# A dense layer and attention projections: from three fp32r matmuls on split operands to plain fp32 on four tiles of 32 columns

## The chip, the cores and the metric

The kernel runs on one core of one Trainium2 chip. The metric is the device time of one execution in microseconds (us), the median of several runs. The two kernels are "before" and "after". TensorE (PE) does the matmuls, VectorE (DVE) and ScalarE (ACT) work element by element, GpSimd (POOL) does small arithmetic and issues some transfers, and SyncE (SP) issues the weight loads.

## What is computed

A trunk of two layers on one sequence of 256 tokens with 1024 channels, everything in float32:

```python
mod_all = einsum('bd,lde->lbe', silu(c), w_mod) + b_mod     # adaLN: 6 vectors of 1024 for each layer
h = rms_norm(x, norm_g[i, 0]) * (1 + scale1) + shift1
y = pool_mixer(h)                  # layer 0
y = diff_attention(h)              # layer 1: h @ w_qkv (1024 x 3072), 8 heads, ..., @ w_o (1024 x 1024)
x = x + gate1 * rms_norm(y, norm_g[i, 1])
h = rms_norm(x, norm_g[i, 2]) * (1 + scale2) + shift2
y = (silu(g) * u) @ w_down         # layer 0: g, u = split(h @ w_gu); D_FF = 2816, the dense layer
y = moe_swiglu(h)                  # layer 1: top 2 of 8 experts, each 3584 wide
x = x + gate2 * rms_norm(y, norm_g[i, 3])
```

The change concerns three parts: the dense layer (`ffn_w_gu`, `ffn_w_down`), attention's input projections (`w_qkv`), and its output projection (`w_o`).

## The kernel before, in words

**Order of the work.** The head computes four pieces of layer 0's adaLN on TensorE (20 units of `w_mod`, `head_units`, L1889) together with the pooling mixer. Then come the dense layer in 11 steps of 256 channels of D_FF, attention with its projections, the router, and the eight experts. The order on each engine is written out by hand; engines meet at semaphores.

**Weight units.** All weights ahead of the experts come in units of 1 MB (128 x 2048 floats, two transfers each) into the buffer `raw`, which has `RAW` = 6 slots. The SP queue issues them in one fixed order (`load`, L530); a unit's load waits until the unit six places ahead of it has been done (`unit_done`). Besides the 20 of the head there are 22 units of gate and up, 11 of the down projection, 12 of queries, keys and values, 4 of the output projection, and 28 later adaLN units, which VectorE multiplies by silu(c) and adds up in `rows` (`gemv_unit`, L1259, two operations a unit): 20 during the dense layer and 8 during the input projections (`FFN_MODS`, `QKV_MODS`). A gate and up unit has 4 of the 8 blocks of 128 input channels and 256 columns of each of the two.

**Splitting.** A float32 operand a is split in two fp32r parts: ScalarE writes the high part (`high`, L860, into `whi`), VectorE subtracts (`low`, L1250, into `wlo`, and counts `unit_done`). Three slots (`SPL` = 3) hold split units. The activations are split likewise: the normalized input into `thi` and `tlo` (L943, L1370 and `modulate_tile`, L975, `low_pair`, L1467), the product of silu and up into `ahi` and `alo`. TensorE then makes each product of three matmuls:

```python
pe.matmul(out, a_hi, b_hi, start=start, stop=False, ...)   # L1873
pe.matmul(out, a_hi, b_lo, start=False, stop=False, ...)   # L1874
pe.matmul(out, a_lo, b_hi, start=False, stop=stop, ...)    # L1875
```

For gate and up (`ffn_gate_up`, L2013), queries and keys (`qkv_group`, L2108) the weights are stationary, 128 x 128, and the input of 256 tokens moves; a product has 256 columns. A step of gate and up is 8 channel blocks x 2 x 2 = 32 products, a group of queries or keys 32 as well. For the down projection (`ffn_down`, L2035, `down_tile`, L2063), the values (L2125 and `last_values`, L2147) and the output projection (L2222) the activation of 128 tokens is stationary and 512 columns of the weights move; these are 8 products a step, 16 for each half of the values, and 32 for the output projection. Step s of the dense layer is gate and up of chunk s+1 and then down of chunk s.

**Around it.** Sixteen bf16 matmuls of zeros clear the down banks after the first step (`zero_bank`, L1877), and 24 keep TensorE busy just before the dense layer (`keep_clock`, L1884). `row_sum` (L1854) adds up a row of `rows` over the partitions with two fp32 matmuls of 512 columns; that of shift 3 (`row_sum(1, 3)`, L2106) stands ahead of the values. The norm ahead of attention ends in full transposes (`turn_normalized`, L2093), whose results ScalarE scales and shifts. In attention TensorE alternates scores, transposes of the weights, the last values' matmuls and the products with the values (L2196 to L2219). `project_low` (L1514) makes the low part of the output weights; the first at the end of the input projections, the other three after the last heads. GpSimd waits for them all (L774) before it clears the experts' sums in HBM (L781).

**Experts.** The ring of 16 slots for expert weights (`ring`, L299) is laid over `raw`, the split buffers and others; loads into it start as the slots become free (L601 to L622). The experts already use plain fp32: the 96 gathered tokens are stationary, 32 at a time, and each of four column tiles of the array (`tile_out`, L358) reads its own quarter of the weights as moving columns: 448 for gate and up (L2359, L2370), 256 for down (L2384). A gate or an up pass is 8 x 3 x 4 = 96 matmuls, a down pass 14 x 3 x 4 = 168; there are 16 of each, and after the last down pass the results are scattered. `gather` (L2307) opens the stage.

Of the kernel before, what the change touches and what calls it, by code (L numbers as in the profile page):

```python
# [34 lines left out]
RAW = 6  # L35
SPL = 3
UNIT = 2048
FC = 256
NCF = FF // FC
# [16 lines left out]
FFN_MODS = [[], [(1, 0, 0), (1, 0, 1)], [(1, 0, 2), (1, 0, 3)], [(1, 1, 0), (1, 1, 1)], [(1, 1, 2), (1, 1, 3)],  # L56
            [(0, 5, 0), (0, 5, 1)], [(0, 5, 2), (0, 5, 3)], [(1, 2, 0), (1, 2, 1)], [(1, 2, 2), (1, 2, 3), (1, 3, 0)],
            [(1, 3, 1), (1, 3, 2), (1, 3, 3)]]
QKV_MODS = [[], [(1, 4, 0), (1, 4, 1)], [(1, 4, 2), (1, 4, 3)], [(1, 5, 0), (1, 5, 1)], [(1, 5, 2), (1, 5, 3)], []]

QKV_ORDER = (4, 0, 1, 2, 3, 5)

R_FFN, Q_FFN = len(HEAD), 0


HT_PARTS = KC
# [4 lines left out]


def ffn_steps():

    r, q, n, steps = R_FFN + 2, 2, 0, []
    for s in range(NCF - 1):
        steps.append((s, r, q, FFN_MODS[s], n))
        r, q, n = r + 3 + len(FFN_MODS[s]), q + 3, n + len(FFN_MODS[s])
    return steps, r, q, n


FFN_STEPS, R_LAST_DOWN, Q_LAST_DOWN, N_QKV_MODS = ffn_steps()
R_QKV, Q_QKV = R_LAST_DOWN + 1, Q_LAST_DOWN + 1
R_GROUP = [R_QKV + 2 * g + sum(len(m) for m in QKV_MODS[:g]) for g in range(6)]
R_WO, Q_WO = R_GROUP[5] + 2, Q_QKV + 12
R_MOE, Q_MOE = R_WO + 4, Q_WO + 4
# [18 lines left out]
ROW_ORDER = [[2, 5], [3, 2, 4, 5]]  # L105

ROW_BANK = [[None, None, 0, None, None, 2], [None, None, 0, 2, 6, 6]]
# [69 lines left out]
def build_trunk(nc, x, c, w_mod, b_mod, norm_g, pool_w, pool_scale, w_qkv, w_o, subln_g, lambda_vecs,  # L177
# [10 lines left out]
    with ExitStack() as ctx:  # L188
# [6 lines left out]
        def early(name, shape, dt=F32):  # L195
            return before_experts.enter_context(nc.sbuf_tensor(name, shape, dt))


# [3 lines left out]
        with ExitStack() as at_first:  # L202
            ring_w = at_first.enter_context(nc.sbuf_tensor("ring_w", [P, 2 * SPL, UNIT], F32))
        whi = sb("whi", [P, SPL, UNIT], F32R)
        wlo = sb("wlo", [P, SPL, UNIT], F32R)
# [5 lines left out]
        thi = sb("thi", [P, UNIT], F32R)  # L211
        tlo = sb("tlo", [P, UNIT], F32R)
        with ExitStack() as at_first:
            act_in = at_first.enter_context(nc.sbuf_tensor("act_in", [P, GROUPS * QUARTER], F32))
        ahi = sb("ahi", [P, 512], F32R)
        alo = sb("alo", [P, 512], F32R)
# [30 lines left out]
        thi3 = thi[:, :].rearrange("p (k s) -> p k s", k=KC)  # L247
        tlo3 = tlo[:, :].rearrange("p (k s) -> p k s", k=KC)
# [3 lines left out]
        last_hi, last_lo = thi[:, 0:512], tlo[:, 0:512]  # L252
# [5 lines left out]
        actf = tmp[:, 512:1024]  # L258
# [20 lines left out]
        before_experts = ExitStack()  # L279
        rows = early("rows", [P, 7, D])  # L280
        scr = early("scr", [P, 6 * D])
        ysb = early("ysb", [P, T, D])
        gain = early("gain", [P, 2, D])
        before_experts.close()
        whx0 = sb("whx0", [P, UNIT], F32R)
        wlx0 = sb("wlx0", [P, UNIT], F32R)
        sb("row4", [P, D])
        whx1 = sb("whx1", [P, UNIT], F32R)
        whx2 = sb("whx2", [P, UNIT], F32R)
        sb("scr_mid", [P, 2 * D])  # L290
        sb("scr_end", [P, UNIT])
        wlx1 = sb("wlx1", [P, UNIT], F32R)
        wlx2 = sb("wlx2", [P, UNIT], F32R)


        o_hi = [whx1[:, :]] + [whi[:, (Q_WO + i) % SPL, :] for i in range(SPL)]
        o_lo = [whx0[:, :]] + [wlo[:, (Q_WO + i) % SPL, :] for i in range(SPL)]
        halves = rows[:, :, :].rearrange("p r d -> p (r d)")
        ring = [raw[:, (R_MOE + i) % RAW, :] for i in range(RAW)] + [halves[:, 5 * D:7 * D]]  # L299
        for i in range(SPL):  # L300
            ring += [ring_w[:, h * SPL + (Q_WO + i) % SPL, :] for h in range(2)]
# [15 lines left out]
        hv = tmp[:, 0:UNIT]  # L317
        hv3 = hv.rearrange("p (k s) -> p k s", k=KC)

# [64 lines left out]
        hi_ready = sem("hi_ready")  # L384
# [19 lines left out]
        first_hi = sem("first_hi")  # L404
        first_lo = sem("first_lo")
# [8 lines left out]
        ht_v = sem("ht_v")  # L414
# [24 lines left out]
        ht_hi = sem("ht_hi")  # L439
        ht_lo = sem("ht_lo")  # L440
# [15 lines left out]
        f_ahi = sem("f_ahi")  # L456
        f_alo = sem("f_alo")
        qkv_ready = sem("qkv_ready")
        values_lo = sem("values_lo")
# [10 lines left out]
        ot_hi = sem("ot_hi")  # L470
        ot_lo = sem("ot_lo")
# [50 lines left out]

        block = ctx.enter_context(nc.Block())
# [5 lines left out]
        def _(sp):  # L529
            def load(r, rounds, halves):  # L530
# [5 lines left out]
                dst = raw[:, r % RAW, :]  # L536
                for view, src in halves(dst):
                    sp.dma_start(view, src).then_inc(raw_loaded[r % RAW], 16)
# [8 lines left out]
            def gu_unit(w, width, chunk, kh):  # L547

                def halves(dst):
                    v = dst.rearrange("p (k g j) -> p k g j", k=4, g=2)  # L550
                    src = w.rearrange("(k p) f -> p k f", p=P)
                    for g in range(2):
                        yield v[:, :, g, :], src[:, kh * 4:kh * 4 + 4, bass.ds(chunk * FC + g * width, FC)]
                return halves
# [18 lines left out]
            for r, (g, pair) in enumerate(HEAD):  # L573
                load(r, 0, mod_unit(0, g, pair))
# [5 lines left out]

            w_gu, w_dn = ffn_w_gu[0], ffn_w_down[0]
            load(R_FFN, 0, gu_unit(w_gu, FF, 0, 0))
            load(R_FFN + 1, 0, gu_unit(w_gu, FF, 0, 1))

            for s, r, _, mods, _ in FFN_STEPS:
                load(r, 0, gu_unit(w_gu, FF, s + 1, 0))
                load(r + 1, 0, gu_unit(w_gu, FF, s + 1, 1))
                for i, mod in enumerate(mods):
                    load(r + 2 + i, 0, mod_unit(*mod))
                load(r + 2 + len(mods), 0, down_unit(w_dn, s))  # L590
            load(R_LAST_DOWN, 0, down_unit(w_dn, NCF - 1))

            for g in range(6):
                for kh in range(2):
                    load(R_GROUP[g] + kh, 0, col_unit(w_qkv[0], QKV_ORDER[g] * 512, kh))
                for i, mod in enumerate(QKV_MODS[g]):
                    load(R_GROUP[g] + 2 + i, 0, mod_unit(*mod))
            for u in range(4):
                load(R_WO + u, 0, col_unit(w_o[0], u % 2 * 512, u // 2))

            def experts(ps_no):  # L601
                u0 = ps_no * NE * EXPERT_UNITS

                def unit(m, e, later, last, src):

                    i = m % RING
                    if ps_no == 0 and m < RING and not last:
                        if i < RAW:
                            sp.wait_ge(unit_done, R_MOE + i - RAW + 1)
                        elif i == RAW:  # L610
                            sp.wait_ge(unit_used, Q_WO + 1)
                        elif i < RAW + 1 + 2 * SPL:
                            sp.wait_ge(unit_used, Q_WO + 2 + (i - RAW - 1) // 2)
                        elif i == RAW + 1 + 2 * SPL:
                            sp.wait_ge(gated, 2 * T + 2)
                        elif i == RAW + 2 + 2 * SPL:
# [1860 lines left out]
```

## Time and profile before

| | |
|---|---|
| median of 3 runs | 1281.88 us (1278.13 to 1283.09) |
| span of the profiled execution, first to last instruction | 1281.1 us (the page gives no other time for it) |
| mean granted clock of TensorE | 0.993 |
| TensorE busy | 1254.9 us (98%) |
| VectorE busy, ScalarE busy | 377.8 us (29%), 214.9 us (17%) |
| moved by DMA | 477.49 MB, mean 373 GB/s |

The profile is of one execution. A busy TensorE is the union of its matmuls, whose ends are modelled; start times are recorded, so the length of a stage or the distance of two starts is the surer measure. Lines L... are those of the kernel before. In a row of the groups by line, "x480" is the number of records and the number after the comma the mean length of one in ns.

### The profile page before, as it was taken

How to read it: one execution, taken by the hardware profiler on the slowest of the kernel's cores; microseconds unless marked ns; L12 is line 12 of the kernel's file. 1: busy time of each engine (PE TensorE's matmuls, PEld its weight loads, DVE VectorE, ACT ScalarE, POOL GpSimd, SP SyncE). 2: the span in 40 equal slices, each digit the busy share in tenths (PEclk: the TensorE clock that was granted, in tenths of full speed). 3: DMA queues.
4: the chain of work that ended last, by engine and by line, in shares of the span. 5: the costliest groups of instructions: out<-in, count | busy, mean ns of one | idle time of the engine just before them, and what ended most of it. 6: DMA issues, size and time to landing. Idle time of an engine off the chain costs nothing.

```text
span 1281.1 us, 31424 instructions
## 1 busy us (share of the span) xinstructions
PE 1254.9 (98%) x14709; PEld 783.7 (61%) x14709; DVE 377.8 (29%) x584; ACT 214.9 (17%) x321; POOL 110.1 (9%) x134
## 2 busy tenths in 40 slices
PE   6899999999999999999999999999999999999997
PEld 3589999989775355545455454554545555454555
DVE  0367877979873110101101011110101201011012
ACT  2353334474742000000000000000000000000001
POOL 2330000010030000020010010002001000200100
PEclk9899999999999999999999999999999999999999
DMA  9998998959369999999999999999999999999980
GB/s 373 387 363 293 325 327 309 374 189 392 150 215 421 424 424 424 424 405 423 425 405 424 424 411 408 424 410 403 424 420 397 421 424 409 405 424 418 397 356 36
DMA packets 114056, 477.49 MB, mean 373 GB/s; under 512 B 10944, under 2 KB 37280, under 8 KB 113792
## 3 DMA queue, kind: packets, MB, share of 16 engines
q1 hardware_dynamic: 106112, 457.29, 89.0%
q0 software_dynamic: 7664, 17.87, 4.5%
q8 instruction: 117, 1.92, 0.5%
q10 hardware_dynamic: 144, 0.26, 0.1%
q14 instruction: 19, 0.16, 0.0%
HBM read 465.79 MB, written 11.16 MB: 372 GB/s over the span
## 4 chain that ended last, share of the span: by engine, by line
PE 95%; DVE 2%; POOL 1%; ACT 1%; issue 0%; DMA 0%; DVEq 0%; ACTq 0%; POOLq 0%
PE ps L2384 23%; PE ps L2370 23%; PE ps L2359 23%; PE ps L1873 7%; PE ps L1874 7%; PE ps L1875 7%; PE ps L1897 2%; PE ps L1988 1%; PE ps L1857 1%; DVE wlo L1518 1%; PE ps L2168 1%; PE ps L1933 0%; DMA scr<-onehot_in 0%; PE ps L1962 0%; PE ps L2313 0%
## 5 line engine op out<-in xcount | busy, mean ns | idle before, releaser
L1745 DVE TENSOR_TENSOR act_in<-act_in,ps 128x1344 f32<-128x1344 f32 x16 | 24.9, 1554 | 526.8 <-PE ps L2370 526.8
L1873 PE MATMUL ps<-thi,whi 128*128 128x256 f32 x480 | 136.0, 283 | 0.7 <-DVE wlo L1367 0.7
L1874 PE MATMUL ps<-tlo,whi 128*128 128x256 f32 x480 | 135.8, 283 | 0.0
L1875 PE MATMUL ps<-thi,wlo 128*128 128x256 f32 x480 | 135.8, 283 | 0.0
L2359 PE MATMUL ps<-raw,turned_in 128*32 128x448 f32 x1296 | 123.7, 539 | 0.0
L2370 PE MATMUL ps<-ring_w,turned_in 128*32 128x448 f32 x1248 | 120.6, 539 | 0.0
L2384 PE MATMUL ps<-ring_w,turned_act 128*32 128x256 f32 x2016 | 117.2, 379 | 0.0
L2384 PE MATMUL ps<-raw,turned_act 128*32 128x256 f32 x2016 | 115.5, 379 | 0.0
L1183 ACT ACTIVATE act_in<-ps 128x1344 f32<-128x1344 f32 x16 | 20.7, 1292 | 548.6 <-PE ps L2359 548.6
L2384 PEld LDWEIGHTS ps<-raw,turned_act 128*32 128x32 f32 x2016 | 82.5, 110 | 33.4 <-issue 3.5
L1253 DVE TENSOR_TENSOR wlo<-raw,whi 128x2048 fp32r<-128x2048 f32 x41 | 92.9, 2289 | 32.8 <-ACT whi L866 32.8
L2359 PE MATMUL ps<-ring_w,turned_in 128*32 128x448 f32 x1056 | 102.6, 539 | 0.0
L2384 PEld LDWEIGHTS ps<-ring_w,turned_act 128*32 128x32 f32 x2016 | 81.2, 110 | 30.2 <-issue 3.1
L2370 PE MATMUL ps<-raw,turned_in 128*32 128x448 f32 x1008 | 96.2, 539 | 0.0
L1873 PEld LDWEIGHTS ps<-thi,whi 128*128 128x128 f32 x480 | 92.1, 192 | 1.3 <-DVE wlo L1367 0.9
L1874 PEld LDWEIGHTS ps<-tlo,whi 128*128 128x128 f32 x480 | 92.1, 192 | 0.4
L1875 PEld LDWEIGHTS ps<-thi,wlo 128*128 128x128 f32 x480 | 92.1, 192 | 0.0
L2359 PEld LDWEIGHTS ps<-raw,turned_in 128*32 128x32 f32 x1296 | 49.8, 110 | 68.7 <-issue 67.8
L2370 PEld LDWEIGHTS ps<-ring_w,turned_in 128*32 128x32 f32 x1248 | 47.4, 110 | 65.9 <-issue 65.9
L866 ACT ACTIVATE whi<-raw 128x2048 fp32r<-128x2048 f32 x43 | 81.1, 1908 | 38.1 <-PE ps L1875 38.1
L816 POOL DMA_INDIRECT expert_sum<-scr,to_row x21 | 33.4, 1589 | 609.3 <-ACT scr L1197 605.0
L2384 PE MATMUL ps<-rows,turned_act 128*32 128x256 f32 x1008 | 85.0, 379 | 0.0
(327 smaller groups left out, 1333.9 us busy)
## 6 DMA issues: line engine op xcount, KB each, us to landing
raw<-moe_w_gu SPq DMA_DIRECT2D x96, 896.0 KB, 12.8
ring_w<-moe_w_gu SPq DMA_DIRECT2D x96, 896.0 KB, 12.8
raw<-w_mod SPq DMA_DIRECT2D x96, 512.0 KB, 6.0
rows<-moe_w_gu SPq DMA_DIRECT2D x48, 896.0 KB, 12.7
raw<-moe_w_down SPq DMA_DIRECT2D x48, 896.0 KB, 13.8
ring_w<-moe_w_down SPq DMA_DIRECT2D x48, 896.0 KB, 13.4
raw<-ffn_w_gu SPq DMA_DIRECT2D x44, 512.0 KB, 5.3
rows<-moe_w_down SPq DMA_DIRECT2D x24, 896.0 KB, 13.1
```

Source lines behind the costliest of these rows:

```text
L816: pool.indirect_dma_start(acc_dram[ps_no].rearrange("r (j d) -> (r j) d", j=4), bass.IndirectOffsetOnAxis(ap=to_row[:, g:g + 1], axis=0), ...
L866: act.activation(whi[:, q % SPL, :], raw[:, r % RAW, :], ACT.Copy).then_inc(hi_ready, 1)
L1183: act.activation(act_3, gate_up_ps(0), ACT.Silu).then_inc(e_sg, 1)
L1253: dve.tensor_tensor(wlo[:, q % SPL, :], raw[:, r % RAW, :], whi[:, q % SPL, :].bitcast(F32), ALU.subtract).then_inc(unit_done, 1)
L1745: dve.tensor_tensor(act_3, act_3, gate_up_ps(1), ALU.mult).then_inc(e_act, 1)
L1873: pe.matmul(out, a_hi, b_hi, start=start, stop=False, skip_group_check=check)
L1874: pe.matmul(out, a_hi, b_lo, start=False, stop=False, skip_group_check=check)
L1875: return pe.matmul(out, a_lo, b_hi, start=False, stop=stop, skip_group_check=check)
L1897: mm = pe.matmul(tile_out(j, HEAD_BANK[g], 0, 256), silu_c[:, k:k + 1].broadcast_to([P, 32]), raw[:, r % RAW, kk * D + 256 * j:kk * D + 25 ...
L2359: mm = pe.matmul(tile_out(j, g, 0, QUARTER), g_t[:, k, 32 * g:32 * g + 32], w[:, QUARTER * j:QUARTER * j + QUARTER], start=(k == 0), stop= ...
L2370: mm = pe.matmul(tile_out(j, 3 + g, 0, QUARTER), g_t[:, k, 32 * g:32 * g + 32], w[:, QUARTER * j:QUARTER * j + QUARTER], start=(k == 0), s ...
L2384: mm = pe.matmul(tile_out(j, *out_ps(g, alone), 256), act_t[c % 2][:, (BLOCKS * g + f) * 32:(BLOCKS * g + f) * 32 + 32], ring[(m + d) % RI ...
```

## The change

- `RAW` = 12 slots of units; `SPL`, `whi`, `wlo`, `thi`, `tlo`, `ahi`, `alo` and all splitting by ScalarE and VectorE go. The input stands once, in float32 (`ht`), the product of silu and up in `acts` with two buffers.
- Each product is four plain fp32 matmuls, one for each tile of 32 columns of the array, with 32 columns of the stationary operand each; all four read the same moving operand and write 32 partitions each of the same bank.
- Gate and up are loaded 512 columns at a time: a unit is 2 blocks of input channels by 512 columns of each. A chunk of four units (two for the last, of 256) serves two steps; its units are free after the second. TensorE's order in the dense layer becomes gate and up of step s, then down of s - 1. The zeroing goes, since the down banks start with their first product.
- One list (`UNITS`) gives the order of loads. A unit's load waits for the use of the unit twelve places ahead. Twelve of the 28 late adaLN units come during the dense layer, sixteen after it.
- ScalarE scales and shifts half of the turned input at the start of the dense layer and VectorE the other half; of the second tile ahead of attention VectorE takes the last four blocks.
- `row_sum(1, 3)` moves from ahead of the values to between the two tiles of the output projection. `keep_clock` ahead of the dense layer has 8 matmuls for 24. GpSimd clears the experts' sums after `ot_ready` 4 (the last turned heads) instead of after the last low part.
- Ring of the experts: still 16 slots, of which 12 lie in `raw`; the other four are in `rows` and `scr`. The slot in rows 5 and 6 waits for `col_ready` 8 and `gated` 4.

The experts' own code, the head, the router, the attention of the heads and the end of the kernel stay as they are.

```diff
-RAW = 6
-SPL = 3
+RAW = 12
+FW = 512
...
+LATE_MODS = [(l, g, pair) for l, g in ((0, 5), (1, 0), (1, 1), (1, 2), (1, 4), (1, 3), (1, 5)) for pair in range(4)]
+MODS_AHEAD = {("down", 1): 2, ("down", 2): 1, ("gate_up", 2, 0): 2, ("down", 3): 2, ("gate_up", 3, 0): 1,
+              ("down", 5): 2, ("gate_up", 4, 0): 2, ("col", 1, 0): 4, ("col", 2, 0): 4, ("col", 3, 0): 4, ("wo", 0): 4}
+def unit_order():
+    weights = chunk_units(0) + [("down", 0)]
+    for chunk in range(1, N_CHUNK):
+        weights += chunk_units(chunk) + [("down", s) for s in (2 * chunk - 1, 2 * chunk)]
+    weights += [("col", g, kh) for g in range(6) for kh in range(2)] + [("wo", u) for u in range(4)]
...
                 if r >= RAW:
-                    sp.wait_ge(unit_done, r - RAW + 1 + rounds * RAW)
+                    used_at(sp, UNITS[r - RAW])
...
                         elif i == RAW:
-                            sp.wait_ge(unit_used, Q_WO + 1)
-                        elif i < RAW + 1 + 2 * SPL:
-                            sp.wait_ge(unit_used, Q_WO + 2 + (i - RAW - 1) // 2)
+                            sp.wait_ge(col_ready, 8)
+                            sp.wait_ge(gated, 2 * T)
...
-            pool.wait_ge(unit_done, R_WO + 4)
+            pool.wait_ge(ot_ready, 4)
...
+            for k in (0, 1, 4, 5):
+                modulated(k)
...
+            for k in (2, 3, 6, 7):
+                part = slice((k % 2) * S, (k % 2) * S + S)
+                dve.tensor_scalar(ht3[:, k, :], ps[:, 4 + k // 2, part], modc[:, 2, k:k + 1], modc[:, 3, k:k + 1],
+                                  ALU.mult, ALU.add).then_inc(ht_vec, 1)
...
-                pe.matmul(out, a_hi, b_hi, start=start, stop=False, skip_group_check=check)
-                pe.matmul(out, a_hi, b_lo, start=False, stop=False, skip_group_check=check)
-                return pe.matmul(out, a_lo, b_hi, start=False, stop=stop, skip_group_check=check)
...
+            def by_columns(b, c0, n, w, src, start, stop):
+
+                for j in range(4):
+                    mm = pe.matmul(tile_out(j, b, c0, n), w[:, 32 * j:32 * j + 32], src, start=start, stop=stop, skip_group_check=True)
+                return mm
...
-            keep_clock(0, 24)
+            keep_clock(0, 8)
...
+            gate_up(0)
+            for s in range(1, NCF):
+                gate_up(s)
+                if s < NCF - 1:
+                    down_tile(s - 1, 0)
+                    down_tile(s - 1, 1).then_inc(unit_used, 1)
...
-            row_sum(1, 3)
...
+                    pe.wait_ge(row_done, done_rank(1, 2))
+                    row_sum(1, 3)
```

## Rows read from the trace of the kernel before

**Rows 1.** The page: busy time (part 1) and the last chain by engine (part 4).
```profile
PE 1254.9 (98%) x14709; PEld 783.7 (61%) x14709; DVE 377.8 (29%) x584; ACT 214.9 (17%) x321; POOL 110.1 (9%) x134
...
PE 95%; DVE 2%; POOL 1%; ACT 1%; issue 0%; DMA 0%; DVEq 0%; ACTq 0%; POOLq 0%
```
**Rows 2.** Windows by stage: start:end, length, busy by engine, granted clock, DMA share, GB/s.
```profile
86.10:250.50 164.40, 164.40 (x1178) 155.78 (x1177) 129.14 (x95) 65.17 (x48) 2.05 (x4) 1.00 0.93 326
...
394.10:1269.40 875.30, 875.30 (x11940) 458.47 (x11940) 96.14 (x170) 28.89 (x34) 55.98 (x45) 1.00 0.99 404
```
**Rows 3.** TensorE in order of time, first dense step: start, us, line, tiles.
```profile
73.64 0.28 PE L1874 MATMUL ps<-tlo,whi 128*128 128x256 f32 x1
...
84.92 0.28 PE L1875 MATMUL ps<-thi,wlo 128*128 128x256 f32 x1
85.04 1.07 PE L1880 MATMUL ps<-zeros 128*128 128x128 bf16 x16
```
**Rows 4.** Windows: two steps of the dense layer.
```profile
97.70:114.68 16.98, 16.98 (x121) 16.02 (x121) 12.98 (x9) 6.76 (x5) 0.00 (x0) 1.00 0.76 257
...
182.60:199.60 17.00, 17.00 (x121) 16.02 (x121) 13.23 (x10) 6.75 (x5) 0.00 (x0) 1.00 0.91 311
```
**Rows 5.** Groups by line: line, engine, operation, count, busy us, mean ns, idle before.
```profile
L1873 PE MATMUL ps<-thi,whi 128*128 128x256 f32 x480 | 136.0, 283 | 0.7 <-DVE wlo L1367 0.7
...
L2384 PEld LDWEIGHTS ps<-ring_w,turned_act 128*32 128x32 f32 x2016 | 81.2, 110 | 30.2 <-issue 3.1
...
L1267 DVE SCALAR_TENSOR_TENSOR rows<-raw,silu_c,rows 128x1024 f32<-128x1024 f32 x28 | 36.0, 1285 | 1.0
...
L1873 PE MATMUL ps<-whi,ahi 128*128 128x512 f32 x80 | 31.7, 396 | 0.0
...
L1873 PE MATMUL ps<-whi,thi 128*128 128x512 f32 x64 | 26.5, 414 | 0.0
...
L1873 PE MATMUL ps<-whx,thi 128*128 128x512 f32 x8 | 3.6, 456 | 0.4 <-DVE tlo L1599 0.4
```
**Rows 6.** The chain that ended last, in order of time: start, us, what.
```profile
28.66 0.87 PE ps L1962 x4
...
250.49 1.72 PE ps L1857 x4
...
331.53 0.43 PE ps L1873
...
394.08 3.81 PE ps L2313 x32
...
471.20 18.13 PE ps L2384 x336
489.33 18.04 PE ps L2359 x192
```
**Rows 7.** All engines in order of time, just before the dense layer.
```profile
71.35 0.17 DVE L1357 TENSOR_TENSOR modc<-ps,cols 128x8 f32<-128x8 f32 x1 [2.89 <-PE ps L1913]
...
71.61 0.51 ACT L947 ACTIVATE thi<-tmp,modc 128x256 fp32r<-128x256 f32 x1 [0.96 <-DVE modc L1357]
```
**Rows 8.** DMA: page part 6, two early windows, all transfers up to 400 us.
```profile
raw<-ffn_w_gu SPq DMA_DIRECT2D x44, 512.0 KB, 5.3
...
0.00:60.00 60.00, 47.06 (x371) 28.24 (x371) 10.75 (x19) 16.67 (x30) 18.02 (x32) 0.94 0.97 379
60.00:70.00 10.00, 9.14 (x84) 5.65 (x84) 3.56 (x10) 3.17 (x5) 5.40 (x6) 0.66 1.07 390
...
DMA packets 55111, 124.96 MB, mean 312 GB/s; under 512 B 4160, under 2 KB 27808, under 8 KB 54951
```
**Rows 9.** In order of time, output projection: its low parts, and TensorE's last matmul.
```profile
357.51 0.74 DVE L1599 SCALAR_TENSOR_TENSOR tlo<-ps,subln,thi 128x512 fp32r<-128x512 f32 x1
...
361.67 4.48 DVE L1518 TENSOR_TENSOR wlo<-raw,whi 128x2048 fp32r<-128x2048 f32 x2
...
383.33 0.39 PE L1875 MATMUL ps<-whi,tlo 128*128 128x512 f32 x1
```

More of the change, by code:

```diff
@@ new lines, in unit_order @@
+def unit_order():
[3 more added lines that the diff above has]
+    weights += [("col", g, kh) for g in range(6) for kh in range(2)] + [("wo", u) for u in range(4)]
+    mods = iter(LATE_MODS)
+    order = [("mod", 0, g, pair) for g, pair in HEAD]
+    for unit in weights:
+        order += [("mod",) + next(mods) for _ in range(MODS_AHEAD.get(unit, 0))]
+        order.append(unit)
+    return order
@@ new lines, in use_order @@
+def use_order():
+    order = []
+    for s in range(NCF):
+        if s % 2 or s == NCF - 1:
+            order += chunk_units(s // 2)
+        if 0 < s < NCF - 1:
+            order.append(("down", s - 1))
+    order += [("down", NCF - 2), ("down", NCF - 1)]
+    return order + [("col", g, kh) for g in range(6) for kh in range(2)] + [("wo", u) for u in range(4)]
+UNITS = unit_order()
+UNIT_NO = {unit: r for r, unit in enumerate(UNITS)}
+USED = {unit: q + 1 for q, unit in enumerate(use_order())}
@@ new lines, with mods_by_step @@
+MOD_DONE = {unit: n + 1 for n, unit in enumerate(u for u in UNITS if u[0] == "mod")}
+R_MOE, Q_MOE = len(UNITS), len(USED)
+assert R_MOE == len(USED) + len(MOD_DONE)
+def mods_by_step():
+    steps, n = {}, 0
+    for unit in UNITS:
+        count = MODS_AHEAD.get(unit, 0)
+        if unit[0] == "gate_up":
+            step = 2 * unit[1]
+        elif unit[0] == "down":
+            step = unit[1] + 1
+        else:
+            step = NCF
+        steps.setdefault(step, []).extend(LATE_MODS[n:n + count])
+        n += count
+    return steps
@@ L69 @@
+DVE_MODS = mods_by_step()
 EDGE = max(WINDOWS)
 BAND = P + EDGE
[L73 to L85, printed above, removed]
@@ L86 @@
-R_MOE, Q_MOE = R_WO + 4, Q_WO + 4
 PRE = 16
@@ L438, in build_trunk @@
         ht_ps = sem("ht_ps")
-        ht_hi = sem("ht_hi")
-        ht_lo = sem("ht_lo")
+        ht_act = sem("ht_act")
+        ht_vec = sem("ht_vec")
         ht32_ready = sem("ht32_ready")
@@ L529, in _, with load @@
         def _(sp):
-            def load(r, rounds, halves):
+            def load(unit, halves):
+                r = UNIT_NO[unit]
                 if 3 <= r < RAW:
@@ L534, in load @@
                 if r >= RAW:
-                    sp.wait_ge(unit_done, r - RAW + 1 + rounds * RAW)
-                dst = raw[:, r % RAW, :]
-                for view, src in halves(dst):
+                    used_at(sp, UNITS[r - RAW])
+                for view, src in halves(slot(unit)):
                     sp.dma_start(view, src).then_inc(raw_loaded[r % RAW], 16)
@@ L751, in _ @@
             for i in range(4):
-                pool.wait_ge(f_ahi, i + 3)
+                pool.wait_ge(f_act, i + 3)
                 part = slice(32 * i, 32 * i + 32)
@@ L1010, in _ @@
             square_residual(0)
-            high(R_QKV + 1, Q_QKV + 1)
             square_down_half(1)
@@ new lines, in gate_up @@
+            def gate_up(s):
+                chunk, part = divmod(s, 2)
+                width, units = chunk_width(chunk), chunk_units(chunk)
+                n = KC // len(units)
+                for i, unit in enumerate(units):
+                    loaded_at(pe, unit)
+                    w = slot(unit).rearrange("p (k g j) -> p k g j", k=n, g=2)
+                    for kk in range(n):
+                        k = i * n + kk
+                        if s == 0 and (k // 2) % 2 == 0:
+                            pe.wait_ge(ht_act, 2 * (k // 4) + k % 2 + 1)
+                        elif s == 0:
+                            pe.wait_ge(ht_vec, 2 * (k // 4) + k % 2 + 1)
@@ L2064, in down_tile @@
+                    if part or s == NCF - 1:
+                        mm.then_inc(unit_used, 1)
+                    elif i == len(units) - 1:
+                        mm.then_inc(gu_ps, 1)
+            def down_tile(s, t):
+                pe.wait_ge(f_act, s + 1)
+                loaded_at(pe, ("down", s))
+                w = slot(("down", s))
                 for half in range(2):
                     for jj in range(2):
-                        a = slice(jj * S + t * P, jj * S + t * P + P)
```

479 lines of the change are left out of this document (140 added, 339 removed).

## The prediction

> **What bounds the kernel now.** I read the busy shares and the chain of waits first. TensorE is busy for 1254.9 of 1281.1 us and carries 95% of the chain that ended last [rows 1]; no DMA wait is in that chain. The windows by stage then say where those microseconds lie: the expert stage takes 875.3 us and the dense layer's steady part 164.4 us, and in both TensorE is busy in every microsecond [rows 2]. The DMA share of the dense layer is high too (0.93 at 326 GB/s), so one must ask which of the two sets the pace. The records of TensorE answer: in the first step it starts a 256-column matmul every 0.120 us without a gap (94 intervals from 73.64 to 84.92 us) [rows 3]. The step keeps its length (16.98 and 17.00 us) although the DMA share of two steps is 0.76 and 0.91 [rows 4]. So TensorE's own work sets the dense layer's time, and the splits on ScalarE and VectorE and the loads lie beside it. What decides is therefore the cost of one matmul product before and after.
>
> I call a product what a group of three split matmuls computes: 128 contracted rows by 128 output rows by 256 or 512 columns. There are 480 products of 256 columns (352 of gate and up, 128 of queries and keys) and 80 + 64 + 8 = 152 of 512 columns (88 of the down projection, 32 of the values, 32 of the output projection), by the counts of the line of the first matmul of each three [rows 5]. Now: 3 x 0.12 = 0.360 us, and, from the step, (16.98 - 32 x 0.360)/8 = 0.683 us.
>
> **The new product.** It becomes four plain fp32 matmuls on tiles of 32 columns. This form is already in the expert stage. The chain has 18.13 us for 336 records of the down line with 256 columns, and 18.04 us for 192 records of the gate line with 448 columns [rows 6]. An expert's down pass is 168 matmuls in the code and a gate pass 96, so one fp32 matmul is two records, and takes 107.9 and 187.9 ns of the stream. The difference, 80.0 ns for 192 columns, is 0.417 ns a column and leaves 1.2 ns for everything else: the stream is bound by its columns, four tiles at once, and the weight loads are hidden. At 512 columns that gives 214.6 ns. Four of each: 0.432 us and 0.858 us a product. Rows that aren't tiled agree: the row sums' 1.72 us for two fp32 matmuls of 512 columns is 0.86 each, and the pooling's 0.87 us for two of 256 is 0.435 [rows 6]. So tiles in fp32 are no faster than the whole array in fp32; the three fp32r matmuls are cheaper in both shapes.
>
> - 256 columns: 480 x (0.432 - 0.360) = **+34.6 us**.
> - 512 columns: 152 x (0.858 - 0.683) = **+26.6 us**.
>
> Bounds: no fixed cost at all (0.427 and 0.853) takes 3 us off; the untiled rows (0.435 and 0.86) add 2. I take the tiled rows, since theirs is the very form. All of this is on the path: nothing of TensorE's work in these stages has cover now.
>
> **A rule that speaks against it.** The expert rows show weight loads of tiles hidden behind matmuls in flight. The Trainium skill says the contrary for this form (TensorE: Matmul & The Clock Gate, Measured speedup vs the span model): a weight load overlaps matmuls in flight only if its row group differs, and tiles of 32 columns all use every row group. By that rule each product would show at least one load in the open, and the time would be that of the second rival below; the trace disagrees, with 1.2 ns left over a matmul.
>
> **Changes of tile shape.** The first split matmul after the scores, which use the rows of the array in halves, takes 0.43 us of the chain [rows 6] where its like take a third of 0.683: 0.2 us for a change of shape. Tiled projections now alternate with full transposes and row sums: about eight more changes in attention, six around the norm ahead of it, three in the output projection. 17 x 0.15, a little under that one row, = **+2.5 us** (nothing to 0.2 each: 0 to 3.4).
>
> **What leaves the path.** At the start of the dense layer come VectorE's shift columns (71.35), ScalarE's high part (71.61), then the low parts up to the first matmul at 73.4 [rows 7]. Now ScalarE writes the input directly: 71.61 + 0.5 + some 0.1 for the hand-over is 72.2, so **-1.2 us**. ScalarE and VectorE halve the eight parts, one in 0.5 us, and each feeds four products, 1.7 us: no wait. Are the weights there? A first chunk is now four units, not two. The DMA moved 379 GB/s up to 60 us and 390 after [rows 8], so 27.4 MB by 72 us; 20 adaLN units, x, the pooling's tables and four dense units are 27.6 MB. The fourth is just late, but wanted 10 us later. The sixteen zeroing matmuls go: 1.07 us with the tail of the last [rows 3], **-0.9 us** of the stream. The shorter warm-up (8 for 24) lies in the wait, and costs 0 to 2 us if the granted clock, 0.66 in the ten us up to 70 [rows 8] and 1.00 in the dense layer [rows 2], rises later.
>
> The row sum of shift 3 (1.7 us) moves from the start of the value matmuls to between the output projection's two tiles: -1.7 there, +1.7 here, and 0.2 of waiting for ScalarE's first column part, which it covered: **+0.2 us**. In the output projection the first matmul, at 358.4, waits for the low part (0.74 us from 357.51), and later ones for the weight splits of 2.2 us each from 361.67 [rows 9]. But 32 x 0.683 of products, 1.7 of a row sum and 1.0 of eight transposes are 24.6 of the 25.2 us to 383.6. So only 0.6, and perhaps 0.2 of the start, come back: **-0.8 us**. GpSimd's clearing of the sums, six DMA issues in its queue ahead of tile 0's roots, waited for the last split; it now waits for the last turned heads and lies under the matmuls. What is late next is tile 1, whose squares follow its last matmul by the same steps as now: 10.5 us to the gather at 394.1 [rows 6].
>
> All other splits on ScalarE and VectorE: nothing, as they lie beside TensorE now. GpSimd's waits on ht_lo and f_ahi become waits on ht_vec and f_act, which come earlier, so nothing queued behind them is later. TensorE's new waits, for adaLN units at three row sums, are for units that VectorE has added up steps before; behind VectorE's additions in a step stands only the product of silu and up, and TensorE has the next gate and up pass, 13.8 us, before it needs that.
>
> **Loads.** The SP queue issues in order, so a late slot holds all behind it. The tightest place: chunk 2's second to fourth unit take slots that are freed in step 3, each 3.5 us apart, the last about 7 us before step 4 begins, and it is wanted 10 us into step 4; landing takes 5.3 us [rows 8]. So no wait. Per step of 20.7 us there are three weight units and one or two adaLN units, at most 5.2 MB, or 250 GB/s, below the 326 of now. Sixteen adaLN units come after the dense layer instead of eight; VectorE takes 16 x 2 x 1.285 = 41 us [rows 5] for them, beside 69 us of values and groups, so the first row maximum, queued behind them, isn't held. The ring's slot in rows 5 and 6 now waits on the SP queue for the norm ahead of attention, long past by then. Before the experts eight units of the ring are in place instead of six, with the remaining eight wanted 18 us after the gather. The stage itself is unchanged: 875.3 us.
>
> **Sum:** 34.6 + 26.6 + 2.5 - 1.2 - 0.9 + 0.2 - 0.8 = +61.0 us on a span of 1281.1, which gives 1342.1. The median of the runs, 1281.88, is 0.8 above the span, so I forecast **1343 us**, 4.8% slower. A measurement of this kernel tells about 0.5% from no change.
>
> **Rivals.**
> - *The four tiles share the stream (faster).* In the expert stage each tile reads its own moving columns; now all four read the same ones. If the columns of the four cost less because of that, a product gets cheaper. It has to come under 0.82 of my price (61.2 of 338 us) to reach no change; at half price the 632 products take 169 us instead of the 276 of now, and the time would be about 1282 - 107 = 1175, were there no other bound; 125 MB up to 400 us [rows 8] at the 404 GB/s of the expert stage [rows 2] want 309, so about 1197. Against it: single fp32 matmuls of the whole array, with one moving stream, also take 0.86 [rows 6]. Chance 0.03; 0.01 more for a price that ends within 0.5%.
> - *Weight loads in the open.* One load of a tile (0.110 us [rows 5]) a product: 632 x 0.11 = +70, so 1413. Against it: the expert rows. 0.02.
> - *Loads come late at chunk boundaries.* Four chunks of up to four units, freed only in a chunk's second step. If each costs 4 us: 16 us, so 1359. For it: DMA share 0.93 now; against: slack as worked out. 0.05.
> - *The change doesn't do what it says*, some products staying split: nothing speaks for it; below 0.01.
>
> **How the numbers follow.** The forecast has 0.89. Its own bounds: prices of products -3 to +2, shapes -2.5 to +1, start and clock -0.5 to +3, attention 0 to -3 if VectorE's chain rather than TensorE sets some of it, output projection -1 to +3: 1333 to 1352 as they combine, widened to 1330 and 1357 for part of the late loads. Faster 0.03, within 0.5% 0.01, slower 0.96.
>
> **What would show it.** The page should have by-column matmuls of 256 columns at 379 ns a record, 480 x 4 x 2 = 3840 records, steps of 20.7 us in the dense layer, the gather at about 455 us, an expert stage of 875 us, and ScalarE and VectorE at less than half in the dense layer. Steps of 17 us or fewer would break the price of a product; TensorE idle behind raw's DMA would mean the loads; a longer expert stage would mean the ring.

## The result and the profile after

The kernel after takes 1341.16 us (median of 4 runs, 1338.44 to 1344.35), the kernel before beside it 1281.92 (4 runs, 1278.13 to 1283.09). The ratio is 1.0476, with a 95% interval of 1.0451 to 1.0501: 4.8% slower. The forecast was 1343 us, within 1330 to 1357.

The page of the kernel after, busy time (part 1), the last chain by engine (part 4) and one group (part 5):

```profile
PE 1311.0 (98%) x17837; PEld 708.1 (53%) x17837; DVE 250.7 (19%) x494; ACT 111.4 (8%) x239; POOL 110.1 (8%) x134
...
PE 97%; DVE 1%; ACT 0%; DMA 0%; POOL 0%; issue 0%; DVEq 0%; ACTq 0%; POOLq 0%
...
L1743 PE MATMUL ps<-ht,raw 128*32 128x256 f32 x3840 | 209.5, 379 | 0.6 <-ACT ht L956 0.6
```

VectorE lost 127 us of work and ScalarE 103.5 us against before, and TensorE, which carries nearly the whole chain in both kernels [rows 1], gained 56. The windows of the kernel after (start:end, length, then busy by engine, granted clock, DMA share, GB/s), the dense layer's steady part, the two projections and the expert stage:

```profile
109.00:281.60 172.60, 172.60 (x2696) 105.76 (x2685) 31.29 (x33) 4.78 (x8) 2.04 (x4) 1.00 0.66 236
...
308.90:372.80 63.90, 63.90 (x1106) 35.70 (x1104) 42.39 (x36) 6.46 (x9) 0.00 (x0) 1.00 0.91 353
...
406.35:439.20 32.85, 32.85 (x273) 10.10 (x273) 11.36 (x27) 6.25 (x12) 10.45 (x17) 1.00 0.88 333
449.40:1324.90 875.50, 875.47 (x11940) 458.02 (x11940) 96.09 (x171) 28.89 (x34) 55.92 (x45) 1.00 0.98 398
```

In the dense layer VectorE is now busy for 31 of 172.6 us where it was for 129 of 164.4, and the loads move 236 GB/s where they moved 326 [rows 2]; TensorE still has no idle microsecond, at the full granted clock. The relief went to engines that TensorE did not have to wait for. The chain of the kernel after has the stretches whole (start, us, what):

```profile
67.65 213.95 PE ps L1743 x3392
281.61 1.91 PE ps L1726 x4
...
308.86 63.97 PE ps L1743 x1104
372.83 1.51 PE ps L2011 x16
374.34 1.85 PE ps L1743 x16
376.20 0.85 PE ps L2011 x8
...
406.35 1.85 PE ps L1743 x16
...
439.22 1.03 PE ps L2101 x8
...
449.43 3.81 PE ps L2158 x32
```

The chain of the kernel before at the same places, as far as its rows don't stand in [rows 6]:

```profile
73.42 0.39 PE ps L1873
...
327.56 1.51 PE ps L2168 x16
329.08 0.43 PE ps L1873
...
330.68 0.86 PE ps L2168 x8
...
383.97 1.09 PE ps L2256 x8
```

From the first dense matmul to the gather the kernel before takes 394.08 - 73.42 = 320.66 us and the kernel after 449.43 - 67.65 = 381.78: **+61.12 us**. This stretch is the best gauge here: it leaves out the head, whose length differs from kernel to kernel for another reason (below), while before and two experiments that don't touch TensorE's work after the head repeat it to 0.01 us.

### The profile page after: what moved, and what is told of

Same layout as the page of the kernel before. It is cut to its first block, busy times and chain, and to the rows that moved or that the text cites. A ratio compares the mean times of both kernels' runs of the same rounds, so it can differ in the third digit from the quotient of the medians.

```text
span 1336.6 us, 37480 instructions
## 1 busy us (share of the span) xinstructions
PE 1311.0 (98%) x17837; PEld 708.1 (53%) x17837; DVE 250.7 (19%) x494; ACT 111.4 (8%) x239; POOL 110.1 (8%) x134
## 4 chain that ended last, share of the span: by engine, by line
PE 97%; DVE 1%; ACT 0%; DMA 0%; POOL 0%; issue 0%; DVEq 0%; ACTq 0%; POOLq 0%
PE ps L1743 25%; PE ps L2229 22%; PE ps L2215 22%; PE ps L2204 22%; PE ps L1759 1%; PE ps L1726 1%; PE ps L2011 0%; PE ps L1795 0%; PE ps L1850 0%; DMA scr<-onehot_in 0%; PE ps L1824 0%; PE ps L1860 0%; PE ps L2158 0%; PE ps L1930 0%; PE ps L2169 0%
## 5 line engine op out<-in xcount | busy, mean ns | idle before, releaser
L2204 PE MATMUL ps<-raw,turned_in 128*32 128x448 f32 x2400 | 228.9, 539 | 0.0
L2229 PE MATMUL ps<-raw,turned_act 128*32 128x256 f32 x4032 | 220.7, 379 | 0.0
L2215 PE MATMUL ps<-raw,turned_in 128*32 128x448 f32 x2208 | 210.8, 539 | 0.0
L1743 PE MATMUL ps<-ht,raw 128*32 128x256 f32 x3840 | 209.5, 379 | 0.6 <-ACT ht L956 0.6
L2229 PEld LDWEIGHTS ps<-raw,turned_act 128*32 128x32 f32 x4032 | 158.6, 110 | 63.8 <-issue 6.6
L1743 PEld LDWEIGHTS ps<-ht,raw 128*32 128x32 f32 x3840 | 144.0, 110 | 67.9 <-issue 6.2
L2204 PEld LDWEIGHTS ps<-raw,turned_in 128*32 128x32 f32 x2400 | 92.8, 110 | 127.1 <-issue 125.4
L2215 PEld LDWEIGHTS ps<-raw,turned_in 128*32 128x32 f32 x2208 | 85.2, 110 | 118.3 <-issue 118.3
L1743 PE MATMUL ps<-raw,acts 128*32 128x512 f32 x704 | 77.8, 592 | 0.0
L2215 PE MATMUL ps<-rows,turned_in 128*32 128x448 f32 x648 | 62.8, 539 | 0.0
L1743 PE MATMUL ps<-raw,ht 128*32 128x512 f32 x512 | 57.8, 595 | 0.3 <-ACT ht L975 0.3
L2229 PEld LDWEIGHTS ps<-rows,turned_act 128*32 128x32 f32 x1008 | 43.0, 110 | 16.9
L1743 PEld LDWEIGHTS ps<-raw,acts 128*32 128x32 f32 x704 | 26.6, 110 | 44.4 <-issue 42.6
L2204 PE MATMUL ps<-rows,turned_in 128*32 128x448 f32 x504 | 48.8, 539 | 0.0
```

The costliest lines, as they stand in the source:

```text
L1743: mm = pe.matmul(tile_out(j, b, c0, n), w[:, 32 * j:32 * j + 32], src, start=start, stop=stop, skip_group_check=True)
L2204: mm = pe.matmul(tile_out(j, g, 0, QUARTER), g_t[:, k, 32 * g:32 * g + 32], w[:, QUARTER * j:QUARTER * j + QUARTER], start=(k == 0), stop= ...
L2215: mm = pe.matmul(tile_out(j, 3 + g, 0, QUARTER), g_t[:, k, 32 * g:32 * g + 32], w[:, QUARTER * j:QUARTER * j + QUARTER], start=(k == 0), s ...
L2229: mm = pe.matmul(tile_out(j, *out_ps(g, alone), 256), act_t[c % 2][:, (BLOCKS * g + f) * 32:(BLOCKS * g + f) * 32 + 32], ring[(m + d) % RI ...
```

## The experiments

All times are medians, and each ratio compares with runs of the kernel before on the chip of that experiment: 1280.8 us beside the whole array, the two tiles and the two depths of the head, 1282.8 beside the two prices of a product, the small splits and the two matmuls of three, 1280.8 beside the last kernel, small splits and two matmuls together. The stretch is that from the first dense matmul to the gather.

### One matmul of the whole array in place of four tiles

```diff
-                for j in range(4):
-                    mm = pe.matmul(tile_out(j, b, c0, n), w[:, 32 * j:32 * j + 32], src, start=start, stop=stop, skip_group_check=True)
-                return mm
+                return pe.matmul(ps[:, b, c0:c0 + n], w, src, start=start, stop=stop, skip_group_check=True)
```

> The kernel after, with each product as one fp32 matmul of the whole array (128 stationary columns) instead of four on tiles of 32. Theory (an fp32 product costs its columns, four times 0.417 ns each, whatever the tiles): a product stays at 0.432 and 0.858 us, the time within 5 us of 1341. Rival (the tiles are what hides the weight loads: the pooling's four whole-array products of 256 columns take 1.92 us, 0.48 each): 480 x 0.048 + 152 x 0.045 = +30, so 1371. Second rival (splitting into tiles costs something): faster by over 5 us, at most 1.2 ns x 4 x 632 = 3 us by the rows, so not seen.

Measured: 1340.05 us (1335.54 to 1340.74), ratio 1.0452 (1.0430 to 1.0474). Chain and groups of this kernel:

```profile
72.09 213.99 PE ps L1742 x848
```
```profile
L1742 PE MATMUL ps<-ht,raw 128*128 128x256 f32 x960 | 209.1, 379 | 0.6 <-ACT ht L956 0.6
L1742 PEld LDWEIGHTS ps<-ht,raw 128*128 128x128 f32 x960 | 182.3, 190 | 29.8 <-issue 5.5
```

The same dense work takes 213.99 us as 424 whole matmuls (848 records) and 213.95 us as 1696 tiled ones (3392 records). So four tiles run side by side at the price of one whole matmul, and no better. A whole weight load (190 ns) is as well hidden behind its matmul as four of 32 columns (110 ns each). The stretch is 450.82 - 72.09 = 378.73 us, 3.05 less than with tiles. The difference shows where tiled products alternate with matmuls of the whole array: the row sum takes 1.72 us here and 1.91 in the kernel after, the eight turns (transposes of an activation) 0.87 and 1.02.

### Two tiles of 64 columns

The same place, with `for j in range(2)` and 64 columns a tile.

> The kernel after, with each product as two fp32 matmuls on tiles of 64 columns. Theory (columns set the cost): 1341 within 5 us, dense steps of 20.7 us. Rival (the number of tiles hides the weight loads): between the whole array and four tiles, about 1356 if the whole array comes at 1371.

Measured: 1341.17 us (1340.87 to 1344.71), ratio 1.0478 (1.0459 to 1.0497). Chain:

```profile
70.41 213.97 PE ps L1743 x1696
```

Again the same 214 us, and a stretch of 381.99: two tiles cost what four do, changes of shape included.

### The price of the product alone, in the kernel before

Two lines ahead of the three matmuls of `three`, for the products of 256 columns; the other kernel has 512 in the place of 256. Splits, buffers, loads and order are those of before.

```diff
+                if b_hi.shape[-1] == 256:
+                    return pe.matmul(out, a_hi.bitcast(F32), b_hi.bitcast(F32), start=start, stop=stop, skip_group_check=check)
```

> The kernel before, with all its splits, buffers, order and loads, but each product of 256 columns (gate, up, queries, keys) computed as one plain fp32 matmul of the high parts on the whole array instead of three fp32r matmuls; the low parts' terms are left out. Theory (the price of a product is all there is): 480 x (0.432 - 0.360) = +34.6 us, less up to 2 us at the start: 1313 to 1317 us. Rival (a good part of the 60 us comes from the new order, the chunks of 512 and the buffers, which this kernel doesn't have): clearly less than +30 here.

> The kernel before, but each product of 512 columns (down, values, output projection) computed as one plain fp32 matmul of the high parts on the whole array instead of three fp32r matmuls; the low parts' terms are left out. Theory: 152 x (0.858 - 0.683) = +26.6 us, perhaps 1 to 2 us more or less at the ends of stages: 1305 to 1309 us; and the rises of this kernel and of the one with the 256-column products alone add up to the 60 us of the change within 3 us. Rival (the cost lies in order and buffers): the two add up to clearly less than 50.

Measured: 1315.04 us (1312.55 to 1317.27), ratio 1.0253 (1.0236 to 1.0271), for the 256 columns; 1305.41 us (1303.34 to 1306.75), ratio 1.0188 (1.0171 to 1.0205), for the 512. The chain of the first (start, us, what), two gate and up passes, and the gather:

```profile
107.73 13.81 PE ps L1874 x64
...
126.99 13.81 PE ps L1874 x64
...
428.45 3.81 PE ps L2315 x32
```

and of the second, the down products of two steps:

```profile
93.17 6.87 PE ps L1874 x16
...
111.56 6.87 PE ps L1874 x16
...
414.30 3.81 PE ps L2315 x32
```

A gate and up pass is 64 records and 32 products, and a down pass 16 and 8: a product of 256 columns costs 13.81 / 32 = 0.432 us and one of 512 costs 6.87 / 8 = 0.859, with all splitting still done beside it. The stretches are 355.02 (+34.4) and 345.36 us (+24.7; its first dense matmul at 68.94). Together they are 59.1 of the 61.1 us of the change; less the 0.9 us of zeroing and with the 3.05 of tile shapes it is 61.2. So the price of the product, with 3 us for the tile shapes, is the change's cost, and the order, the chunks of 512 and the twelve slots are not.

### Six units in flight in the head, and twelve in the kernel before

The profiled kernel after begins the dense layer 5.8 us earlier than before, where the forecast had 1.2. Either the deeper ring feeds the head better, or it is chance. The first kernel is the kernel after with this wait added; the second is the kernel before with its 20 adaLN units of the head going round twelve places.

```diff
+                if 6 <= r < 26:
+                    used_at(sp, UNITS[r - 6])
```
```diff
+def place(r):
+
+    return (8, 11)[r - 18] if r in (18, 19) else r % 12 if r < 20 else r % RAW
...
+        def head_raw(r):
+            i = place(r)
+            return raw[:, i, :] if i < RAW else ring_w[:, i - RAW, :]
```

> The kernel after, where units 6 to 25 of the load order also wait for the use of the unit six places ahead, so that the head has six units in flight again; from unit 26 on nothing is changed. My sum left out that the head ends 4.6 to 5.9 us earlier in the kernel after. Theory (the depth of twelve does it: weights arrive without a gap and TensorE's clock isn't let down): the dense layer starts at about 73 us instead of 67.7, the time is 4 to 6 us longer than after, 1346. Rival (chance of where the clock falls in one execution): the start stays below 70 and the time within 2 us of 1341.

> The kernel before, where the 20 units of the head go round twelve slots (six of raw and six of the space of the split parts, which is unused in the head) instead of six; nothing else. Theory (depth of loads in the head): dense layer starts at about 68.5 instead of 73.4, so 1277, ratio 0.996. Rival (chance of the clock): within 1 us of before, ratio 1.000.

Measured: 1341.17 us (1338.28 to 1341.72), ratio 1.0465 (1.0450 to 1.0481), first dense matmul at 70.15 us and a stretch of 381.78; and 1281.80 us (1280.62 to 1283.57), ratio 1.0006 (0.9997 to 1.0015), first dense matmul at 71.53 and a stretch of 320.66. Neither depth moves the time: the theory of the deeper ring fell, although the start of the first kernel lies 0.15 us above the 70 that the rival had named. What goes with the start is the clock. Windows of the head (the number after the engines is the granted clock), of the kernel with 256-column products alone, dense start at 73.43:

```profile
30.00:40.00 10.00, 9.51 (x77) 5.27 (x80) 3.39 (x9) 3.90 (x8) 4.66 (x2) 0.89 1.03 419
40.00:50.00 10.00, 10.00 (x77) 6.73 (x70) 0.00 (x0) 1.49 (x3) 0.79 (x2) 0.77 0.93 352
...
60.00:70.00 10.00, 9.12 (x84) 5.74 (x84) 3.56 (x10) 3.19 (x5) 5.40 (x6) 0.66 1.06 391
```

and of the kernel after, dense start at 67.65:

```profile
30.00:40.00 10.00, 9.51 (x73) 6.06 (x73) 3.39 (x9) 3.06 (x6) 4.67 (x2) 1.00 1.03 419
40.00:50.00 10.00, 10.00 (x85) 7.34 (x87) 1.74 (x2) 1.53 (x4) 0.79 (x2) 1.00 1.03 418
...
60.00:70.00 10.00, 8.89 (x120) 5.58 (x116) 2.07 (x5) 2.31 (x5) 6.18 (x8) 0.86 1.05 407
```

I added up the granted clock of the four windows from 30 to 70 us for each profiled run. "As before" are the kernels with split inputs, "as after" those with `ht`:

| sum of the four clocks | first dense matmul, as before | as after |
|---|---|---|
| 3.31 to 3.32 | 73.42, 73.43, 73.53 | 72.09 |
| 3.49 | 70.97, 71.52, 71.53 | 70.15, 70.41 |
| 3.65 to 3.66 | 68.94 | 67.65 |

Between the means of a row the new start is 1.1 to 1.4 us earlier, with up to 0.6 us between kernels of one row; the rest of the 5.8 us goes with the clock of that one profiled run.

### Were the splits beside TensorE? Small splits, two matmuls of three, and both

The first kernel splits only 64 of the 2048 columns of each weight unit after the first four, on ScalarE (shown) and on VectorE alike; the second leaves out L1874; the third does both. The activations are still split in all three.

```diff
-                act.activation(whi[:, q % SPL, :], raw[:, r % RAW, :], ACT.Copy).then_inc(hi_ready, 1)
+                n = UNIT if q < SPL + 1 else 64
+                act.activation(whi[:, q % SPL, 0:n], raw[:, r % RAW, 0:n], ACT.Copy).then_inc(hi_ready, 1)
...
-                pe.matmul(out, a_hi, b_lo, start=False, stop=False, skip_group_check=check)
```

> The kernel before, with the splits of the weight units cut from 2048 columns to 64 on ScalarE and VectorE once the first units are through; the matmuls, loads and waits stay. The products then use split values that are left over from earlier units, and the branch for overfull experts is never taken: this is what the kernel leaves out. Theory (TensorE's matmuls set the dense layer, the splits lie beside them): 1278 to 1282 us against 1281, the first dense stretch as long as before (177 us). Rival (the splits set the pace of the kernel before, so that leaving them out is where the change should have gained): VectorE loses some 2 us a unit over 35 units, so down to 1281 - 70 = 1210 if all of it was in the open, and below 1265 if a fifth of it was.

> The kernel before with the second matmul of each three left out (high part of the stationary operand by low part of the moving one), so that a product is two matmuls; all splits and loads stay. It leaves that term of the sum out. If TensorE alone had set the dense layer with unlimited cover: 480 x 0.12 + 152 x 0.228 = 92 us less, so 1189 us. My theory says the cover is near: a step of 17.0 us has 13.0 us of VectorE's work and 5.2 MB of loads (13.4 us at 390 GB/s), so a step can't go under about 13.3 us instead of the 11.3 of its matmuls; that gives back some 20 us in the dense layer and some more in the projections: about 1224 us, ratio 0.955. Rival (VectorE or the loads set the pace already): within 1% of before.

> The kernel before with the second matmul of each three left out and the splits of the weight units cut to 64 of 2048 columns as well (so that term of the sum is left out, later products use left-over split values, and the branch for overfull experts is never taken). With two of three matmuls and full splits a dense step took 15.2 us, against 17.0 us for three and 11.3 us of matmuls. Theory (the loop of VectorE's splits and additions, 13 us busy a step, holds it at 15.2): with VectorE's work cut to some 7 us a step, the loads are next, 5.2 MB a step at 390 GB/s = 13.4 us, and the stretch from the first dense matmul to the gather falls from 295.0 us to about 265 to 275, the time to 1226 to 1238 us. Rival (the loads with their six slots hold it at 15.2 already): the stretch stays at 293 to 296 us and the time at 1254 to 1258 us.

Measured, small splits: 1280.58 us (1278.18 to 1280.98), ratio 0.9985 (0.9975 to 0.9995), and a stretch of 391.62 - 70.97 = 320.65 us, the same as before to 0.01; the 2 us by which its median is lower lie outside this stretch. From 97.7 to 180 us VectorE has 33.7 us of work where the kernel before has 63.5 (second row), and TensorE is as long as ever:

```profile
97.70:180.00 82.30, 82.30 (x591) 77.97 (x590) 33.73 (x48) 9.19 (x24) 2.05 (x4) 1.00 0.95 332
...
97.70:180.00 82.30, 82.30 (x580) 77.51 (x580) 63.48 (x49) 33.57 (x25) 2.05 (x4) 1.00 0.91 320
```

So taking the splitting of the weights away gives nothing by itself. That is the half of the change that looks like a gain.

Two matmuls of three: 1255.95 us (1253.70 to 1258.97), ratio 0.9802 (0.9779 to 0.9825), a stretch of 294.97 us. Here my number missed: I had 1224, and TensorE alone would give 1189. ScalarE's high parts of `ahi`, one a step, stand 15.2 us apart (99.62, 114.83, 130.05 us), not 13.3. VectorE in order of time over such a step (start, us):

```profile
115.49 0.69 DVE L1257 TENSOR_TENSOR alo<-tmp,ahi 128x512 fp32r<-128x512 f32 x1 [0.70 <-ACT ahi L959]
117.30 6.70 DVE L1253 TENSOR_TENSOR wlo<-raw,whi 128x2048 fp32r<-128x2048 f32 x3 [1.11 <-ACT whi L866]
124.10 1.29 DVE L1265 SCALAR_TENSOR_TENSOR rows<-raw,silu_c,rows 128x1024 f32<-128x1024 f32 x1
...
130.71 0.69 DVE L1257 TENSOR_TENSOR alo<-tmp,ahi 128x512 fp32r<-128x512 f32 x1 [0.70 <-ACT ahi L959]
```

The window of one such step of the same kernel:

```profile
100.16:115.37 15.21, 11.43 (x68) 10.13 (x67) 13.13 (x9) 6.63 (x7) 0.00 (x0) 0.89 0.95 347
```

VectorE is busy for 13.1 us of it, and in the other 2 it waits for ScalarE (0.70 and 1.11 among them), which the sum of busy times doesn't have. The chain that ended last goes round the same loop in these steps, VectorE's and ScalarE's work alone, without TensorE and without a load:

```profile
114.20 0.61 DVE tmp L1405
...
115.37 1.91 ACT whi L866
...
117.30 6.71 DVE wlo L1253 x3
...
124.10 1.30 DVE rows L1265
```

Both together: 1233.30 us (1232.67 to 1234.33), ratio 0.9629 (0.9612 to 0.9645), a stretch of 345.41 - 73.53 = 271.88 us and steps of 67.42 / 5 = 13.5 us, with the DMA now full (window of five steps) and ScalarE waiting for it where it had waited for TensorE (waits from 90 to 240 us: total, times, longest):

```profile
124.25:191.67 67.42, 61.61 (x409) 56.79 (x408) 35.55 (x51) 9.44 (x25) 1.49 (x3) 0.95 1.05 406
```
```profile
ACT whi L867 <- DMA raw<-ffn_w_gu: 26.2, 15, 2.5
```

So at two matmuls a product VectorE's loop held the steps at 15.2 us, and the loads hold them near 13.5 once it is gone. The kernel before, at 17.0 us a step, has 1.8 us of cover over the first and 3.5 over the second. No run here that computes every term was faster than the kernel before.

## Why the prediction was right, and where its terms were off

By its own terms, in us. The stretches end at the chain's pieces; the last column has the kernels in which only the price of a product changed, 256 columns + 512 columns.

| stretch | before | after | forecast | measured | in the kernels with one edit |
|---|---|---|---|---|---|
| dense layer | 177.07 | 213.96 | +37.0 | +36.9 | 25.2 + 12.6 |
| input projections, to the first scores | 77.07 | 91.22 | +14.0 | +14.15 | 9.2 + 5.2 |
| attention and output projection | 56.41 | 66.39 | +11.2 | +10.0 | 0.0 + 6.8 |
| from there to the gather | 10.11 | 10.21 | 0 | +0.1 | 0.0 + 0.1 |

The forecast of each row is put together from the prediction's terms (dense: 352 x 0.072 + 72 x 0.175 - 0.9; input projections: 128 x 0.072 + 32 x 0.175 - 1.7 for the row sum + 6 x 0.15; the third: 48 x 0.175 + 1.7 + 0.2 + 11 x 0.15 - 0.8); with -1.2 for the start they are the +61.0. The 0.9 us between 25.2 + 12.6 and 36.9 in the dense layer are the zeroing that went.

**What bounds it: right.** The dense layer went on at TensorE's pace in both kernels, and with the splits cut down it moved by no more than 0.01 us.

**The price of a product: right, and shown twice.** 0.432 and 0.859 us, against 0.432 and 0.858 that the expert stage's rows had given, in the changed kernel and in the kernels that have nothing but this edit. The 512-column term was the one that was too large: +24.7 us was measured for the forecast's 26.6, though in the dense layer it is exact (12.6 of 12.6). Of the missing 1.9 us, 1.6 lie in attention and output projection. A pair of these products between two scores takes 330.68 - 329.08 = 1.60 us in before, not 1.37, and 1.91 in the kernel with 512-column products alone: +0.31 for the forecast's 0.35. The output projection, from its first matmul to the router's first, goes from 383.97 - 358.39 = 25.58 us to 404.12 - 373.82 = 30.30: +4.7 for the forecast's 5.6.

**What leaves the path in attention and output projection: too small.** The forecast gave 0.8 us back for waits. Some of before's waits are in no idle time of TensorE, only in its starts, 0.23 us apart as a rule but 0.63 here:

```profile
361.19 0.79 PE L1873 MATMUL ps<-whx,thi 128*128 128x512 f32 x1
361.82 0.39 PE L1874 MATMUL ps<-ahi,thi 128*128 128x512 f32 x1
...
383.97 1.09 PE L2256 MATMUL ps<-consts,hs 128*128 128x128 f32 x8 [0.26 <-DVE hs L1628]
```

That is why this stretch takes +10.0 us and not +11.2. The forecast was 8.4 for products, 1.1 for row sum and waits and 1.65 for shapes; measured are 6.8, 1.1 and, against whole matmuls, 2.05. As an estimate from these runs, the 1.3 us by which the 6.8 fall short of 2.5 for eight pairs and 5.6 for the output projection, and the 0.6 by which the 1.1 falls short of a row sum of 1.7, are some 1.9 us of waits that went.

**Changes of tile shape: the right size, a little small.** +2.5 was forecast and 3.05 is what whole matmuls save, 0.18 for each of the 17: 2.05 of it in attention and output projection (1.65 forecast) and 1.0 in the input projections (0.9). In attention the cost stands behind the pair and not in it, since the pair begins with a change of shape from the scores either way, the very row from which I had taken the 0.2 us [rows 6]. The pair and the transpose behind it, in the kernel after and with whole matmuls:

```profile
387.33 1.85 PE ps L1743 x16
389.18 0.42 PE ps L2024 x2
...
386.77 1.91 PE ps L1742 x4
388.69 0.22 PE ps L2022 x2
```

**The start of the dense layer: right at equal clock** (-1.1 to -1.4 for -1.2), although the profiled run alone shows -5.8. So the gather came at 449.4 us and not at about 455, with the stretch before it as forecast.

**Loads and waits: right.** No stretch of the dense layer waits for a unit, with the DMA share at 0.66, and the expert stage takes 877 us up to the end of the scatter in both kernels. The late-loads rival is out.

**The rivals.** Shared streams would have made the dense layer shorter, and it is 37 us longer. Open weight loads would have added 70; the dense stretch is exact to 0.1 us without them. The rule that spoke for them (the Trainium skill, TensorE: Matmul & The Clock Gate, The mechanism, ahead of the section that the prediction names: loads overlap matmuls in flight only when the row group differs) doesn't hold in these runs: the stationary operand has 128 rows in all three shapes, and with 32, 64 and 128 columns the dense stretch takes 213.95, 213.97 and 213.99 us.

**The sum.** +61.1 us over the stretch, -1.2 at the start at equal clock, and 0.1 in the expert stage, is +60.0 for the forecast's +61.0; the medians of the two kernels differ by 59.2. The 1 us is the attention stretch. That it is so little owes something to luck: there the waits that go were priced over 1 us too low and the changes of shape 0.4 too low, and the two have opposite signs.

## What to carry to other kernels

Before relieving an engine, ask who waits for it: here 231 us of VectorE's and ScalarE's work were taken away, and what paid was TensorE, the one engine without an idle microsecond in the dense layer and the input projections. Three fp32r matmuls on split operands beat plain fp32 here (0.360 to 0.432 us a product at 256 columns, 0.683 to 0.859 at 512), with the splitting fitting beside them, and how well it fits is read from the loop of hand-overs (15.2 us), not from the busy sum (13.1). Compare kernels over a stretch between two fixed pieces of the chain: it repeated to 0.01 us here, where single whole runs of one kernel differ by 5 to 6.

## What was not expected of the hardware

- The granted clock of the first 70 us is another in each kernel's profiled run, with nearly the same work, and lies as a mean between its two levels, 1.2 GHz (0.5) and 2.4 GHz (1.00): in the ten us up to 70 it was 0.66 in four runs and 0.83 to 0.88 in the others. TensorE was busy in all of the ten us up to 50, at 0.77 in one kernel and 1.00 in another. The start of the dense layer moves with it by 4.5 us, which is more than many edits are worth. Why it falls where it does is open.
- With two matmuls of three, TensorE is busy for 11.4 us of a step of 15.2, at a granted clock of 0.89, where the full steps of before have 1.00 [rows 4]. That costs nothing there, since VectorE's loop sets the step. But the same router, from its first matmul to the gather, takes 10.11 us in before, 12.84 with two matmuls of three and 13.83 with small splits as well, at a granted clock of 1.00, 0.73 and 0.64. So 2.7 and 3.7 us of what fewer matmuls win go with a lower clock. The windows, in that order:

```profile
383.97:394.08 10.11, 8.61 (x114) 6.28 (x114) 7.39 (x24) 6.00 (x15) 2.51 (x5) 1.00 1.02 417
...
353.65:366.49 12.84, 11.38 (x114) 8.79 (x115) 7.34 (x24) 5.71 (x13) 2.31 (x5) 0.73 1.02 423
...
331.58:345.41 13.83, 12.60 (x115) 9.60 (x115) 7.36 (x24) 5.72 (x13) 2.31 (x5) 0.64 1.02 422
```
- Tiles of the array are worth nothing in themselves for plain fp32: four of 32 columns, two of 64 and one of 128 give the same time to 0.04 of 214 us. They only add 0.15 to 0.20 us at places where they alternate with matmuls of the whole array (1.72 to 1.91 us for a row sum, 0.87 to 1.02 for eight transposes, 0.22 to 0.42 for two).
